# Feed-forward down products: ScalarE copies and accumulating DMAs instead of VectorE additions

## What is computed

```
def rmsnorm(x, g):
    xf = x.astype(jnp.float32)
    y = xf * lax.rsqrt(jnp.mean(xf * xf, axis=-1, keepdims=True) + NORM_EPS)
    return (y * g.astype(jnp.float32)).astype(x.dtype)

def swiglu(x, w_gate, w_up, w_down):
    return (jax.nn.silu(x @ w_gate) * (x @ w_up)) @ w_down
...
x = x + 0.5 * swiglu(rmsnorm(x, ffn1_norm[l]), ffn1_w_gate[l], ffn1_w_up[l], ffn1_w_down[l])
...  (attention, forgetting attention, gates, w_out)
x = x + 0.5 * swiglu(rmsnorm(x, ffn2_norm[l]), ffn2_w_gate[l], ffn2_w_up[l], ffn2_w_down[l])
return rmsnorm(x, final_norm)
```

## Time and profile before

| | us |
|---|---|
| time, median of 3 runs | 2142.38 (2140.95 to 2144.67) |
| the profiled execution | 2140.0 |
| its span, first to last instruction | 2138.2 |
| TensorE busy | 2097.6 (98%) |
| VectorE busy | 1606.8 (75%) |
| ScalarE busy | 1090.8 (51%) |
| GpSimd busy | 0.2 |
| DMA queue of SyncE, share of the 16 engines' span | 56.1% of it |
| mean granted TensorE clock | 0.996 |

### The profile page before, as it was taken

How to read it: one execution, slowest core, us unless ns; L and a number is a source line. 1 busy time by engine, 2 the same in 40 slices (tenths; PEclk the granted TensorE clock), 3 DMA queues, 4 the chain that set the end, 5 groups by cost and what they waited for, 6 DMA issues and landing times.

```text
span 2138.2 us, 26519 instructions
## 1 busy us (share of the span) xinstructions
PE 2097.6 (98%) x9475; PEld 1728.2 (81%) x9475; DVE 1606.8 (75%) x1613; ACT 1090.8 (51%) x1259; POOL 0.2 (0%) x4
## 2 busy tenths in 40 slices
PE   7999999999999999999999999999999999999997
PEld 5788888888887888888888888878888888888876
DVE  6888888888888744444455555688888889888886
ACT  5545555545555544555454344465555555555553
POOL 0000000000000000000000000000000000000000
PEclk9999999999999999999999999999999999999999
DMA  7556566556566545545445665555565665555652
GB/s 247 187 167 215 177 217 214 182 171 216 177 216 207 167 158 180 188 160 171 158 164 183 204 206 185 189 190 199 162 204 188 216 206 195 166 201 188 220 198 98
DMA packets 204643, 402.88 MB, mean 188 GB/s; under 512 B 8576, under 2 KB 8752, under 8 KB 204464
## 3 DMA queue, kind: packets, MB, share of 16 engines
q1 hardware_dynamic: 202032, 401.64, 56.1%
q10 hardware_dynamic: 2560, 0.55, 0.1%
HBM read 400.06 MB, written 2.10 MB: 188 GB/s over the span
## 4 chain that ended last, share of the span: by engine, by line
PE 93%; DVE 3%; ACT 2%; DMA 1%; issue 1%; SPq 0%; ACTq 0%; DVEq 0%
PE ps L520 21%; PE ps L522 21%; PE ps L521 21%; PE ps L533 6%; PE ps L535 6%; PE ps L534 6%; PE ps L694 3%; PE ps L696 3%; PE ps L695 3%; PE ps L585 1%; DMA raw<-in_ffn_w_gate 1%; DMA raw<-in_ffn_w_up 1%; DVE xres L1283 1%; DVE w_lo L1178 1%; ACT chunk_buf L946 0%
## 5 line engine op out<-in xcount | busy, mean ns | idle before, releaser
L1178 DVE TENSOR_TENSOR w_lo<-raw,w_hi 128x1024 fp32r<-128x1024 f32 x256 | 312.6, 1224 | 312.2 <-ACT w_hi L909 311.9
L909 ACT ACTIVATE w_hi<-raw 128x1024 fp32r<-128x1024 f32 x256 | 269.8, 1059 | 313.0 <-PE ps L522 307.1
L922 ACT ACTIVATE w_hi<-raw 128x1024 fp32r<-128x1024 f32 x300 | 317.8, 1059 | 218.0 <-PE ps L522 97.6
L1199 DVE TENSOR_TENSOR w_lo<-raw,w_hi 128x1024 fp32r<-128x1024 f32 x300 | 366.4, 1221 | 77.3 <-ACT w_hi L922 66.5
L520 PE MATMUL ps<-w_hi,xT_hi 128*128 128x512 f32 x816 | 321.6, 394 | 7.1 <-DVE w_lo L1178 6.7
L522 PE MATMUL ps<-w_hi,xT_lo 128*128 128x512 f32 x816 | 318.6, 390 | 0.0
L521 PE MATMUL ps<-w_lo,xT_hi 128*128 128x512 f32 x816 | 318.3, 390 | 0.0
L520 PE MATMUL ps<-w_hi,hT_hi 128*128 128x512 f32 x576 | 224.4, 390 | 0.0
L522 PE MATMUL ps<-w_hi,hT_lo 128*128 128x512 f32 x576 | 224.1, 389 | 0.0
L521 PE MATMUL ps<-w_lo,hT_hi 128*128 128x512 f32 x576 | 224.1, 389 | 0.0
L922 ACT ACTIVATE w_hi<-sums 128x1024 fp32r<-128x1024 f32 x100 | 106.2, 1062 | 223.0 <-DVE sums L1209 111.8
(11 more groups left out here) (212 smaller groups left out, 3635.6 us busy)
## 6 DMA issues: line engine op xcount, KB each, us to landing
raw<-in_ffn_w_gate SPq DMA_DIRECT2D x88, 1024.0 KB, 5.1
raw<-in_ffn_w_up SPq DMA_DIRECT2D x88, 1024.0 KB, 5.2
raw<-in_ffn_w_down SPq DMA_DIRECT2D x88, 1024.0 KB, 5.1
raw<-in_w_in SPq DMA_DIRECT2D x80, 1024.0 KB, 5.0
raw<-in_w_out SPq DMA_DIRECT2D x16, 1024.0 KB, 5.0
raw<-in_w_proj_dil SPq DMA_DIRECT2D x8, 1024.0 KB, 5.0
raw<-in_w_proj_fox SPq DMA_DIRECT2D x8, 1024.0 KB, 4.9
xres<-in_x SPq DMA_DIRECT2D x4, 512.0 KB, 7.1
```

Of the source, the lines that this page charges most:

```text
L909: nc.scalar.activation(slot_hi(place, offset), raw_half(place, offset), ACT.Copy).then_inc(hi_ready, 1)
L922: nc.scalar.activation(slot_hi(place, offset), src, ACT.Copy).then_inc(hi_ready, 1)
L1178: nc.vector.tensor_tensor(slot_lo(place, offset), raw_half(place, offset), slot_hi(place, offset).bitcast(F32), ALU.subtract).then_inc(lo_ ...
L1199: nc.vector.tensor_tensor(slot_lo(place, offset), step_source(r)[0], slot_hi(place, offset).bitcast(F32), ALU.subtract).then_inc(lo_ready, 1)
```

## The change

In the nine looped steps of each block the four additions leave VectorE. ScalarE instead copies the down product from PSUM, scaled by 0.5, into one half of `gate_buf` (two halves in turn), and GpSimd issues a DMA that adds this half to the columns of `xres` in place. The semaphore `down_copied` counts the copies and `down_added[n]` the DMAs of group n. TensorE waits for the copy instead of the addition. A copy waits until the DMA of two groups before has read its half of `gate_buf`; a DMA waits for the copy and for the DMA of the same columns in the step before. The tenth step and the last down product still add on VectorE, after a wait for the DMAs. On ScalarE the first step is written out ahead of its loop, since its first two copies have nothing to wait for. Each block has 9 x 4 = 36 such copies and DMAs, 72 in all.

```
+        @block.gpsimd
+        def _(pool):
+            pool.memset(f_abs[0:1, 0, 0:1], 0.0).then_inc(down_copied, 1)
+            for j in range(2 * (STEPS - 1)):
+                for n in range(NN):
+                    pool.wait_ge(down_copied, j * NN + n + 2)
+                    if j > 0:
+                        pool.wait_ge(down_added[n], j * 16)
+                    pool.dma_start(xres[:, :, n * CH:(n + 1) * CH], gate_buf[:, n % 2],
+                                   accum_op=ALU.add).then_inc(down_added[n], 16)
...
                             transpose_tokens(hid, 0, T)
 
                             pe.wait_ge(hidden_ready, hid + TT)
-                            pe.wait_ge(added, base)
+                            pe.wait_ge(down_copied, drained)
...
-                    pe.wait_ge(added, base + NN - 1)
+                    if last:
+                        pe.wait_ge(added, base + NN - 1)
+                    else:
+                        pe.wait_ge(down_copied, drained + NN - 1)
...
+                        if not last and o > STEP - DOWN and o % 2 == 1:
+                            n = (o - (STEP - DOWN)) // 2
+                            earlier = f * (STEPS - 1) + (n >= 2)
+                            act.wait_ge(slab_done, place.slab(o + 1))
+                            if not (type(i) is int and i == 0 and earlier == 0):
+                                act.wait_ge(down_added[(n + 2) % NN], i * 16 + earlier * 16)
+                            banks = DOWN_BANKS[n]
+                            nc.scalar.activation(gate_buf[:, n % 2], ps[:, banks:banks + TT], ACT.Copy,
+                                                 scale=0.5).then_inc(down_copied, 1)
                         if last and o == STEP - DOWN + 4:
+                            for n in (2, 3):
+                                act.wait_ge(down_added[n], (f + 1) * (STEPS - 1) * 16)
                             round_hidden(i * TT + HID[f] + TT, last_hi, A)
 
-                with act.Fori(0, STEPS - 1) as i:
+                step(step_place(f), 0, False)
+                with act.Fori(1, STEPS - 1) as i:
                     step(step_place(f, i), i, False)
...
-                        if o > STEP - DOWN and o % 2 == 1:
+                        if last and o > STEP - DOWN and o % 2 == 1:
                             n = (o - (STEP - DOWN)) // 2
+                            dve.wait_ge(down_added[n], (f + 1) * (STEPS - 1) * 16)
                             add_down(place, o + 1, n, DOWN_BANKS[n], 0.5)
```

More of the change, by code:

```diff
@@ L324, in build @@
     combined = sem("combined")
+    down_copied = sem("down_copied")
+    down_added = [sem(f"down_added{n}") for n in range(NN)]
     hi_ready = sem("hi_ready")
@@ L378, in build @@
     out_ready = [sem(f"out_ready{n}") for n in range(NN)]
-    ADDED = {0: 1, "mix": 1 + FF_CHUNKS * NN, 1: 1 + (FF_CHUNKS + NN) * NN}
-    ADDED_ALL = ADDED[1] + FF_CHUNKS * NN
+    ADDED = {0: 1, "mix": 1 + 2 * NN, 1: 1 + (2 + NN) * NN}
+    ADDED_ALL = ADDED[1] + 2 * NN
     AT_BOUNDARY = (0, ADDED["mix"], ADDED[1], ADDED_ALL)
@@ L638, in step @@
                 def step(place, i, last):
-                    hid, base, merged = i * TT + HID[f], i * NN + ADDED[f], (i + f * STEPS) * COMBINED
+                    hid, merged = i * TT + HID[f], (i + f * STEPS) * COMBINED
+                    drained, base = i * NN + (f * (STEPS - 1) * NN + 1), ADDED[f]
                     for o in paired(place, 0, 0):
@@ L682, in ffn @@
                 step(final_step_place(f), STEPS - 1, True)
-                last_down(last_place(f), HID[f] + STEPS * TT, ADDED[f] + STEPS * NN, 1 if f == 0 else None)
+                last_down(last_place(f), HID[f] + STEPS * TT, ADDED[f] + NN, 1 if f == 0 else None)
             def direct_up(place, offset, k0, first, last):
```

## The result

The changed kernel took 2199.3 us (median of 4, 2194.7 to 2202.3) beside 2142.6 for the kernel before: 1.0262 times as long, with an interval from 1.0238 to 1.0286. That is 57 us more, outside the range. The sign and the path were as predicted; the loss was 2.7 times the 21 us of the sum. The profiled execution took 2202.1 us, its span is 2200.3, 62.1 more than before.

A forecast was written before the change was run, and what follows sets the result against it. TensorE's matmuls were taken to bound the kernel, with load 5 close behind at 0.17 us of slack. 18 boundaries x 1.2 us = 21.6, less 0.5, gave +21 on 2142.4: 2163 us, range 2140 to 2192.

The forecast's parts named there:

- the sum: Whole kernel: 18 step boundaries x 1.2 us of TensorE waiting, less 0.5 us, +21 us, giving 2163 us.
- What bounds the kernel: Looped steps: TensorE's matmuls set the time; what load 5 loses beyond 0.17 us of slack, TensorE loses too.
- Additions off VectorE, "Gain: 0": Looped steps: 72 additions, 87.6 us, leave VectorE and gain 0; 0.5 us for the tenth steps.
- "faster": Rival: VectorE is further ahead in every step and the tenth steps lose nothing, some 3 us, 2139 us; chance 0.05.
- Copies on ScalarE: Each of 72 copies out of PSUM takes 1.06 us of ScalarE's idle time; no loss.
- Loads 4 and 5 earlier: Step start: load 4 issued about 1.1 us earlier, load 5 0.15 us, its slack growing from 0.17 to 0.32 us.
- Work of an accumulating DMA, 3.13 us: Each 512 KB addition occupies the DMA engines for 3.13 us for two operand reads, 1.57 if like a plain transfer.
- Start, 2.0 us behind the copy: GpSimd's DMA packets start 2.0 us behind the copy, range 1.5 to 3.5; group 3's near 590.7.
- "Groups 0 to 2 ... have many microseconds to spare": First three additions of a step run in the down product, where engines pause and loads have many microseconds to spare.
- The clock as a rival of 0.08: Rival: load 5 up to 2.9 us late, TensorE waits 2.6 us and its clock falls, 2216 us; chance 0.08.
- the long-wait case: Slow start or addition: waits of 2.6 us plus 1.5 us of low clock at 18 boundaries, 74 us; chance 0.08.
- fits into the gap: Rival: an addition costing 1.57 us and starting within 2.5 us leaves load 5 inside its slack, 2142 us; chance 0.31.

The follow-up runs named there:

- the deferred kernel: Changed kernel, but GpSimd issues the fourth accumulating DMA only after load 5 of the next step has landed: 2130.3 us, 0.9956 of the kernel before.
- the one with the split first: Changed kernel, VectorE's split of slab 10 moved ahead of the two sums that read load 5: 2162.8 us, 1.0098 of the kernel before.
- the kernels without the third addition: Changed kernel with accumulating DMAs cut to 2 KB: the first three (2158.7 us, 1.0075) or only the third (2160.0 us, 1.0098).
- the fourth alone: Changed kernel with its fourth accumulating DMA whole and the first three cut to 2 KB each: 2158.7 us, 1.0075 of the kernel before.
- the plain one: Changed kernel with plain copy DMAs over xres in place of the accumulating ones, sum lost: 2143.4 us, 1.0013 of the kernel before.
- the kernel without additions: Changed kernel without its 72 accumulating DMAs; ScalarE still copies, nothing adds the copies: 2128.4 us, 0.9946 of the kernel before.
- 15 with the split first: Changed kernel, fourth DMA held until load 5 landed, slab 10's split ahead of the sums needing load 5: 2124.6 us, 0.9929 of the kernel before.

## Why the prediction was off

**What bounds the kernel: right, but for the boundary.** What load 5 lost, TensorE lost. The earlier trace rows carried this, and the deferred kernel and the one with the split first have shown it from both sides. That a looped step never waits for VectorE was wrong at the step's boundary, as the next point says.

**Additions off VectorE, "Gain: 0": right for VectorE, wrong for TensorE.** VectorE's busy time fell by 74.5 us and not by 87.6, in part since its instructions overlap (one of 1.21 us is followed by the next 1.13 us later). Relief of VectorE brought nothing (2128.4 us with and without its additions), and at most 4 us in a kernel where load 5 was out of the way. But the same edit frees the banks of groups 2 and 3 sooner, and TensorE waited there at every boundary: 1.5 us of "issue" in 7 waits over eight steps, which I read as no wait at all. It was a wait for `added` ahead of the back edge, without a name, and a third product held back by a matter of tenths. The second was in the prediction's own numbers: it had the addition's end at 590.04 and the copy's at 588.70, and called that "no loss" without looking when the product started. It started right behind the addition:

```profile
590.17 0.49 PE L533 MATMUL ps<-w_hi,xT_hi 128*128 128x512 f32 x1
```

Worth 12 us, and 15 with the split first: no rounding error, and the chance of "faster" (0.05) was too small for it, though the DMAs drowned it.

**Copies on ScalarE: right.** 1.01 us, no loss.

**Loads 4 and 5 earlier: right in kind, smaller.** Load 4 is issued at the step's start, 0.04 us ahead (before 0.68 behind the earlier trace rows): 0.7 us and not 1.1. Load 5 goes out 4.40 us into the step, before 4.43: nothing, instead of 0.15. And the slack did not grow from 0.17 to 0.32 us but was used up: TensorE's third product, and with it all up to the first direct product, came 0.35 us sooner, and load 5 did not.

**Work of an accumulating DMA, 3.13 us: right.** It is 3.15; the plain one, at 1.34, is the lower end that I had at 1.57. That two operands are read is not seen in a trace. The rule that an addition halves the rate (the Trainium skill, Collectives: The Full Stack, "The bandwidth ceiling") agrees in kind; against a plain transfer of the same tiles it was a factor of 2.3.

**Start, 2.0 us behind the copy: right for free engines, too early here.** It was 2.7 in the step shown: GpSimd issued 0.3 us behind the copy's end, and packets followed 2.4 us later. Where load 4 is out of the way, in the kernels without the third addition and in the deferred one, the fourth addition's first packet comes 1.8 us behind the issue (medians of 18), 2.1 behind the copy. The 1 us to the first byte that the Trainium skill gives (DMA: Bandwidth & Descriptors, "Specifications") didn't hold when counted from the start of GpSimd's issue, of which 1.20 us are its own instruction; nor did my lower end that leaned the same way. The copy itself ended 2.17 us into the step (forecast 1.93). The engines were free 7.8 us into it, and not 7.4.

**"Groups 0 to 2 ... have many microseconds to spare": wrong, the step that failed.** The prediction put their cost at nothing; the third addition costs 41 us when it stands ahead of the fourth (2200.0 against 2158.7 us). Groups 0 and 1 do cost nothing. The third addition runs over the boundary, from 542.9 to about 546, with load 4 behind it. With the fourth alone the prediction's sum is nearly met: load 5 is 1.5 us late, as worked out, and there are 29.8 us of waits beside 21.6. The difference is the slack, which was used up (0.15 + 0.35 us in each of 18 steps would be 9 us). That this kernel comes so near the forecast is partly luck, since the gain that was left out makes up for it: 29.8 of waits + 2.9 of busy time - 11.8 = 20.9 us, beside the 21 of the sum. With the third as well load 5 is 2.5 us late. I had added up the collision for one transfer and treated the others as free because their own loads weren't urgent; but the queue behind them was. I can show that the third is needed for it; why it costs load 5 1.1 us, when load 4 itself lands only 0.4 us later (5.55 against 5.14 us into the step, medians), is not settled. The traces point to a backlog that is uneven over the 16 engines, so that a load of which each carries a part waits for the slowest: twice as much of load 6 has gone ahead when load 5 lands, 0.48 MB against 0.23 to 0.25. No run tested it, and no view shows the engines one by one.

**The clock as a rival of 0.08: wrong place.** With waits of 2.7 us it belongs to the main case: 26.4 us, 1.5 per step, which is close to the price that the prediction had taken from the earlier trace rows (1.8 for each of the 15 steps in which the clock fell). The condition was right as well (between 1.15 and 1.89 us the rows were silent; the first waits with a fallen clock are of 1.88 us). Waits of the predicted 1.2 us wouldn't have met it. So errors of 1.0 us in load 5's landing and 0.5 us in the slack were paid at 18 x (1.5 + 1.5) = 54 us, beside 48.0 + 26.4 - 21.6 = 52.8 measured.

**The sum by steps.** Forecast: 18 x 1.2 - 0.5 = 21 us. Measured: 48.0 of waits + 26.4 of clock - 11.8 at the boundaries = 62.6 of span, beside 62.1. The range's upper end, 2192, had counted most of the long-wait case as unlikely and the gain as nothing; it missed the median by 7 us.

**The rivals.** That a DMA of half the work fits into the gap seems to hold for the plain one (1.0013), but that is two errors that cancel: beside the kernel without additions it costs 15 us. That VectorE ahead makes it faster: no, what made it faster were the banks. ScalarE stood still ahead of none of its 72 copies.

## What to carry to other kernels

Work given to DMAs is only as free as the transfer that lands last in a chain with slack. Find it (here load 5, slack 0.17 us), and count every DMA that can be in the engines from one or two transfers ahead of it until it has landed, not only the one that overlaps it. Then let the new DMA wait for that landing: this one wait turned 1.026 into 0.996. And look at short unnamed gaps of the engine that sets the time at a loop's edge: they may be a wait for a bank, and a copy that frees it sooner was worth 12 us here, and 15 once the next thing in line, load 5's slack, was seen to.

## What the runs showed of the hardware that was not expected

- An accumulating DMA of 512 KB within SBUF takes the 16 engines for 3.15 us, a plain one for 1.34, and 5.5 us instead of 3.9 from issue to landing; while it runs, the engines are full at 160 to 213 GB/s, where loads reach some 390. It goes in twice as many packets as the plain one. GpSimd is busy for 1.20 us with each issue.
- Two queues didn't share the engines evenly. Load 5 was issued 1.9 us behind the fourth addition, and from 549.5 to 551.5 its queue got one packet through and the addition's queue 186; the rate rose to 330 GB/s only after it.
- A semaphore wait ahead of a hardware loop's back edge that was met late left a gap of 0.37 us in TensorE's stream, though the third addition had ended 0.6 us before the next matmul. The same wait a few instructions later left none there, and neither did a wait ahead of the edge that was met long before.
- None of 59 stops of up to 1.73 us lowered TensorE's granted clock here, and all of 26 stops of over 2.5 us did, to between 0.50 and 0.66 over the next 4 us, that is, largely 1.2 instead of 2.4 GHz. Between them it went either way.
